# GpSimd splits k's and v's first weight tiles in the opening of a hybrid attention kernel

## The reference, cut to what matters

```
h   = RMSNorm(x) * g_pre                    x is 1024 x 1024, float32
P   = h @ W_in                              columns: q, k, v, z (512 each), then the GLA branch and the gates
A   = stick-breaking attention(q, k, v), 8 heads of 64, strictly causal
B   = gated linear attention, 4 heads
m   = sigmoid(gA) * (A * silu(z)) @ Wo_a + sigmoid(gB) * (rmsnorm(B) * silu(zB)) @ Wo_b
y   = RMSNorm(x + m @ W_out)
```

## Time and profile before

| what | value |
|---|---|
| median of three runs | 792.67 us (792.51 to 793.82) |
| profiled execution, its own time | 793.86 us |
| its span | 792.1 us |
| DVE busy | 582.3 us (74%) |
| ACT busy | 413.5 us (52%) |
| POOL busy | 33.0 us (4%), 30 instructions |

### The profile page before, as it was taken

The page is one execution under the profiler, slowest core; times in us unless marked ns, Lnnn a source line. Parts: engine busy times, 40 slices in busy tenths (PEclk is TensorE's granted clock), DMA queues, the critical chain, the costliest instruction groups (busy, mean ns, idle before and its releaser), DMA issues.

```text
span 792.1 us, 11786 instructions
## 1 busy us (share of the span) xinstructions
PE 781.1 (99%) x4394; PEld 665.4 (84%) x4394; DVE 582.3 (74%) x835; ACT 413.5 (52%) x714; POOL 33.0 (4%) x30
## 2 busy tenths in 40 slices
PE   7999999999999999999999999999999999999997
PEld 6888888888888888899899888888888888888886
DVE  6649897987999798832656777655467777779986
ACT  7546666675667566522615544434343333365443
POOL 1560000000000000020000000000000000000000
PEclk9999999999999999999999999999999999999999
DMA  9772121202201211112111001243433333395222
GB/s 330 247 253 54 28 54 53 53 26 53 53 26 46 54 44 43 32 54 62 38 36 27 29 28 54 93 160 120 146 120 107 106 107 107 108 369 214 107 106 107
DMA packets 72483, 76.31 MB, mean 96 GB/s; under 512 B 3804, under 2 KB 57207, under 8 KB 71928
## 3 DMA queue, kind: packets, MB, share of 16 engines
q1 hardware_dynamic: 72242, 75.45, 29.9%
q10 hardware_dynamic: 198, 0.28, 0.1%
HBM read 55.79 MB, written 15.73 MB: 90 GB/s over the span
## 4 chain that ended last, share of the span: by engine, by line
PE 93%; ACT 2%; DVE 2%; issue 1%; DMA 1%; SPq 0%; DVEq 0%; ACTq 0%
PE pj L708 27%; PE pj L833 6%; PE tr L1002 6%; PE ob L951 5%; PE sc L951 5%; PE ob L781 4%; PE ob L1002 4%; PE pj L1002 4%; PE tr L791 4%; PE sc L1002 3%; PE pj L724 3%; PE pj L814 3%; PE sc L757 2%; PE sc L756 2%; PE ob L1028 1%; PE sc L1028 1%
## 5 line engine op out<-in xcount | busy, mean ns | idle before, releaser
L708 PE MATMUL pj<-h_lo,w_hi 128*128 128x512 f32 x336 | 133.2, 396 | 0.0
L708 PE MATMUL pj<-h_hi,w_lo 128*128 128x512 f32 x336 | 132.1, 393 | 0.0
L708 PE MATMUL pj<-h_hi,w_hi 128*128 128x512 f32 x336 | 132.0, 393 | 0.0
L1691 DVE TENSOR_TENSOR_SCAN surv<-surv,diag 128x128 f32<-128x128 f32 (+3 forms) x64 | 86.4, 1349 | 7.5 <-ACT surv L1182 7.3
L708 PEld LDWEIGHTS pj<-h_hi,w_hi 128*128 128x128 f32 x336 | 63.1, 188 | 12.6
L708 PEld LDWEIGHTS pj<-h_hi,w_lo 128*128 128x128 f32 x336 | 63.2, 188 | 12.4 <-issue 0.3
L708 PEld LDWEIGHTS pj<-h_lo,w_hi 128*128 128x128 f32 x336 | 63.1, 188 | 12.3 <-issue 0.2
L1228 ACT ACTIVATE wt_hi<-tr 128x512 fp32r<-128x512 f32 (+2 forms) x96 | 43.6, 490 | 36.4 <-PE tr L791 35.0
L1628 DVE TENSOR_TENSOR w_lo<-w_raw,w_hi 128x1024 fp32r<-128x1024 f32 x33 | 40.3, 1221 | 23.0 <-ACT w_hi L1124 22.8
L1726 DVE TENSOR_TENSOR wt_lo<-tr,wt_hi 128x512 fp32r<-128x512 f32 (+2 forms) x96 | 50.2, 550 | 7.1 <-ACT wt_hi L1228 6.6
L1695 DVE TENSOR_TENSOR beta<-beta,surv 128x128 f32<-128x128 f32 (+3 forms) x64 | 48.6, 759 | 6.5
(11 more groups left out here) (435 smaller groups left out, 1895.7 us busy)
## 6 DMA issues: line engine op xcount, KB each, us to landing
w_raw<-in_w_in SPq DMA_DIRECT2D x30, 512.0 KB, 3.9
y_scratch<-y_ring SPq DMA_DIRECT2D x28, 256.0 KB, 2.0
graw<-in_w_in SPq DMA_DIRECT2D x14, 512.0 KB, 5.2
y_back<-y_scratch SPq DMA_DIRECT2D x14, 512.0 KB, 5.2
x_t<-in_x SPq DMA_DIRECT2D x8, 512.0 KB, 6.8
wrow<-in_w_out SPq DMA_DIRECT2D x4, 1024.0 KB, 9.0
w_scratch<-wsum SPq DMA_DIRECT2D x4, 1024.0 KB, 5.0
wout_raw<-in_w_out SPq DMA_DIRECT2D x8, 512.0 KB, 8.8
```

The lines of the kernel that those rows point to most:

```text
L708: mm = pe.matmul(pj[bank][:, :], (w_lo if p == 2 else w_hi)[:, slot, k, :], (h_lo if p == 1 else h_hi)[:, k, HALF * h:HALF * h + HALF], st ...
L1691: dve.tensor_tensor_scan(s[:, ::-1], s[:, ::-1], d[:, ::-1], 0.0, ALU.mult, ALU.add)\
```

## The change

For k's and v's first weight tiles (n = 1 and n = 2) both halves of the split move to POOL: a `tensor_copy` into the float32r high part in place of ACT's activation, and a `tensor_tensor` subtraction in place of DVE's. The four instructions stand in POOL's list behind its two fills and ahead of its AFFINE_SELECT and its 16 sums. ACT and DVE keep q's tile, and their other work moves up.

```
@@ POOL, behind the fills of surv and diag
+            for n, (raw, hi, lo, loaded) in ((1, (w_raw[:, 1, :, :], w_hi[:, 1, :, :], w_lo[:, 1, :, :], raw_loaded[1])),
+                                             (2, (w2_raw[:, :, :], w2_hi[:, :, :], w2_lo[:, :, :], raw2_loaded))):
+                pool.wait_ge(loaded, 16)
+                pool.wait_ge(hi_done, n)
+                pool.tensor_copy(hi, raw).then_inc(hi_done, 1)
+                pool.wait_ge(hi_done, n + 1)
+                pool.wait_ge(lo_done, n)
+                pool.tensor_tensor(lo, raw, hi.bitcast(F32), ALU.subtract).then_inc(lo_done, 1)
@@ ACT, behind h_high(range(KT))
-            high_part(1, 1, 1, None, None)
-            row_norms(range(4, 7))
-            act.wait_ge(raw2_loaded, 16)
-            act.activation(w2_hi[:, :, :], w2_raw[:, :, :], ACT.Copy).then_inc(hi_done, 1)
-            row_norms([7])
+            row_norms(range(4, 8))
@@ DVE, behind h_low(range(KT))
-            low_part(1, 1)
-            norm_rows(range(4, 7))
-            dve.wait_ge(hi_done, 3)
-            dve.tensor_tensor(w2_lo[:, :, :], w2_raw[:, :, :], w2_hi[:, :, :].bitcast(F32),
-                              ALU.subtract).then_inc(lo_done, 1)
-            norm_rows([7])
+            norm_rows(range(4, 8))
```

## The result

The changed kernel takes 800.57 us (median of four runs, 799.83 to 802.26), the kernel before 792.87 beside it. The ratio is 1.0097, with a 95% interval of 1.0085 to 1.0109: 7.7 us slower. The forecast was 801.8 us.

A forecast was written before the change was run, and what follows sets the result against it. TensorE, busy 99%, was taken to bound the kernel. Terms -0.3 (norm wait), +7.75 (stall) and +1.7 (clock) gave 9.15 us on the 792.67 us median: 801.8 us, range 796.5 to 804.5.

The forecast's parts named there:

- The gap that bounds: On TensorE, busy 99%: k's weight split is on time by some 0.3 us; whatever comes later is paid in full.
- The ISA step: Build-inserted instruction on POOL, 12.15 us idle before AFFINE_SELECT; claimed to move behind k's CAST, 13.5 to 25.65 us.
- the likeliest case: Whole-kernel forecast of 801.8 us, with its own range 799.7 (ISA step at 10 us) to 804.5.
- K's CAST: POOL's copy making k's high part: waits for q's high part, runs 12.4 to 13.5 us, POOL ahead of DVE.
- K's TENSOR_TENSOR: POOL's subtraction making k's low part: 2.5 us, ending at 28.15; one of DVE's norms might be in the way.
- The stall: TensorE before the 25th projection matmul, k's first needing the low part: start at 28.25 instead of 20.50, +7.75 us.
- The clock: TensorE's granted clock at half when k's matmuls begin and for a while after: +1.7 us, between 0 and 2.0.
- X's last norm: DVE's norm of x's last tile comes earlier, so TensorE's 0.33 us wait for it goes: -0.3 us.
- Queued behind: POOL's 16 sums start 5.25 us later, but ACT's entry into the main loop no longer waits: costs nothing.
- A step bound to a fixed moment: Rival, 5 in 100: POOL's step ends at 15.65 whoever asks, so both splits are on time; 792.4 us.
- A step of AFFINE_SELECT alone: Rival, 4 in 100: POOL's splits on time, 16 sums 12.5 us later, TensorE idle at about 55 us; 806.6 us.
- The shorter step: Rival, 9 in 100: POOL's step takes half, 6.1 us, stalling TensorE 1.7 to 2.45 us; about 795.3 us.

## Why the prediction was right

*The gap that bounds.* That k's split had 0.3 us of slack and all beyond is paid in full held: of the 7.68 us by which v's first matmul is late, 7.43 are left at the last matmul, and the median changed by 7.70.

*The ISA step.* Right in kind: two kernels in which all four instructions stay on POOL and the step comes earlier have no loss (in the second ACT's early wait is gone as well). No profile has a record of the ISA row itself; it is tied to the idle time by its place in the lists alone. Wrong in size: 12.15 us expected, 9.54 measured in the profile (8.64 in the second), the largest error of the sum and below the 10 us that the likeliest case allowed. The one instance I had was the longest of eleven. The Trainium skill, "GPSIMD Engine Reference" (section on instruction dispatch), gives about 6 us for the first call after a load of new code; no profile here shows it so short, the shortest being 7.36 us.

*K's CAST.* Expected 12.4 to 13.5, measured 13.19 to 14.61. It did not wait for q's high part but for its own raw weights; I had not asked when k's raw data land, only that they were there when ACT read them at 17.86. DVE's subtraction for q ran from 12.49 to 13.72, so that of the CAST's 1.42 us 0.53 lie beside it and 0.89 behind it. In each of the six profiles with this CAST behind the fills it ends 0.88 to 0.90 us behind DVE's subtraction; with nothing in its way it took 1.03, near the fill (0.95) as taken. The collision was foreseen, but with POOL first as the likelier; DVE was first.

*K's TENSOR_TENSOR.* 2.5 expected, 2.33 measured. It had another victim: DVE's norm of x's last tile takes 2.72 us in place of 0.75. It ends 0.55 us behind the end of POOL's subtraction, so I read it as blocked until then:

```profile
24.32 2.72 DVE L1627 TENSOR_SCALAR x_t<-x_t,stats 128x1024 f32<-128x1024 f32 x1
```

TensorE didn't need it before 34 us.

*The stall.* 7.75 us expected. The 25th matmul was due at 20.58 (20.35 + 0.23) and started at 26.54: 5.96. The difference of 1.8 is the step (-2.6), the CAST (+1.1), the subtraction (-0.2) and the start (-0.1).

*The clock.* +1.7 expected; 24 matmuls took 34.18 - 26.54 = 7.64 in place of 5.45: +2.2, above the upper bound of 2.0 that I had set.

*X's last norm.* -0.3 expected; the turned slices took 35.84 - 34.18 = 1.66 us in place of 28.16 - 25.95 = 2.21: -0.55. I had counted only the wait that the profile names, and the weight loads had waited 0.25 more.

Sum: 5.96 + 2.19 - 0.55 = 7.6, against 9.15 expected. That the forecast came within 1.2 us owes something to luck: the step was priced 2.6 us too long, and the late CAST and the dearer clock made up 1.6 of it. *Queued behind:* the 16 sums started 3.8 us later and ACT entered the main loop without waiting for them, as said.

*The rivals.* A step bound to a fixed moment is out: it ended at 15.65 before and at 24.16 now. A step of AFFINE_SELECT alone is out: TENSOR_TENSOR pays it. The shorter step was partly true and gave the right direction of the error, but the 6.1 us that it was priced at is shorter than any step measured.

## What to carry to other kernels

Work moved to an idle engine brings what that engine must do first. Look in the built order for instructions that nobody wrote, and in the trace for an idle time put down to "issue" ahead of the first instruction of a kind; keep a cheap instruction of that kind early, in a place that nobody waits for, the other engines' waits on the neighbours included. An instance of such a cost taken from one profile is one draw: its spread over eleven profiles here was 7.4 to 12.2 us.

With the step out of the way the change is worth nothing that can be measured (0.9992 to 1.0010): it relieves two engines that TensorE waited for by 0.5 us.

## What the hardware showed that was not expected

- A CAST and a MEMSET on POOL ran without the step, TENSOR_TENSOR and AFFINE_SELECT did not. A 128 x 1024 CAST took 1.03 us where nothing blocked it.
- The half clock lasted for 10 matmuls behind an idle time of 5.8 us, for 9 behind one of 5.0 and for 13 behind one of 3.7: the shortest of the three stalls cost most. The clock came back 4.4 us behind k's first matmul in the changed kernel's first profile (31.0 and 26.54) and 5.8 us behind it with the loads of W_out held back (29.1 and 23.31).
- The first projection matmul came anywhere from 13.4 to 14.8 us in eleven of the profiles (the twelfth is the one in which ACT waited for the fill), with the same instructions of TensorE ahead of it. Two profiles are compared from that matmul on, not from the start of the span.
